# Neighbourhood attention on items of two heads by 16 grid columns, with the outputs read by the merge through a view

## The reference

```python
def row_fn(r):
    ...
    s_loc = jnp.einsum('bhqd,bhiqjd->bhqij', qr, kn) * scale + bias
    s_ctx = jnp.einsum('bhqd,bhmd->bhqm', qr, kc) * scale
    ...
    s = jnp.concatenate([s_loc.reshape(bsz, hh, wq, kh * NA_KW), s_ctx], axis=-1).astype(jnp.float32)
    p = jax.nn.softmax(s, axis=-1).astype(v.dtype)
    ...
    return jnp.einsum('bhqij,bhiqjd->bhqd', p_loc, vn) + jnp.einsum('bhqm,bhmd->bhqd', p_ctx, vc)
```

## Time and profile before

| | us |
|---|---|
| median of 3 runs | 2396.49 (2395.66 to 2397.57) |
| the profiled execution's own time | 2396.7 |
| its span, first to last instruction | 2394.9 |
| PE busy | 2350.3 (98%) |
| DVE busy | 1614.3 (67%) |
| ACT busy | 965.6 (40%) |
| POOL busy | 126.5 (5%) |
| mean granted clock of PE | 0.997 |

### The profile page before, as it was taken

How to read it: one execution, slowest core, us unless ns; L and a number is a source line. 1 busy time by engine, 2 the same in 40 slices (tenths; PEclk the granted TensorE clock), 3 DMA queues, 4 the chain that set the end, 5 groups by cost and what they waited for, 6 DMA issues and landing times.

```text
span 2394.9 us, 33087 instructions
## 1 busy us (share of the span) xinstructions
PE 2350.3 (98%) x13244; PEld 2034.2 (85%) x13244; DVE 1614.3 (67%) x2135; ACT 965.6 (40%) x1453; POOL 126.5 (5%) x158
## 2 busy tenths in 40 slices
PE   7999999999999999999999999999999999999998
PEld 4988988998877888898889888889889896998996
DVE  7677658856378545686766786766688556678656
ACT  2422356743136322353224464224567323544443
POOL 1000001101100000010000010000011010000000
PEclk9999999999999999999999999999999999999999
DMA  8655555652133344444456575456556243676763
GB/s 281 182 170 177 187 193 165 194 179 68 50 110 89 123 132 135 156 134 158 163 172 202 175 220 166 158 172 197 185 184 204 90 133 100 214 253 197 223 202 123
DMA packets 466300, 396.26 MB, mean 165 GB/s; under 512 B 34132, under 2 KB 418148, under 8 KB 465892
## 3 DMA queue, kind: packets, MB, share of 16 engines
q1 hardware_dynamic: 450704, 386.98, 51.3%
q10 hardware_dynamic: 15444, 7.17, 1.1%
HBM read 392.93 MB, written 1.17 MB: 165 GB/s over the span
## 4 chain that ended last, share of the span: by engine, by line
PE 89%; DVE 7%; issue 1%; DMA 1%; ACT 1%; ACTq 0%; POOL 0%; SPq 0%; DVEq 0%
PE ps L1648 27%; PE ps L1650 27%; PE ps L1649 27%; DVE wl L1031 2%; PE ps L1945 1%; PE ps L2021 1%; PE ps L2000 1%; PE ps L2104 1%; DVE st L1099 1%; DMA araw<-in_ada_w 1%; PE ps L1755 1%; PE ps L1926 1%; PE ps L2009 1%; ACT wh L590 1%; DVE acc L1046 0%
## 5 line engine op out<-in xcount | busy, mean ns | idle before, releaser
L1031 DVE TENSOR_TENSOR wl<-raw,wh 128x1024 fp32r<-128x1024 f32 x560 | 681.4, 1221 | 561.3 <-ACT wh L590 559.5
L590 ACT ACTIVATE wh<-raw 128x1024 fp32r<-128x1024 f32 x560 | 591.7, 1059 | 1147.4 <-PE ps L1650 1078.9
L1648 PE MATMUL ps<-hh,wh 128*128 128x256 f32 (+1 forms) x2720 | 883.9, 325 | 1.1 <-DVE hl L1204 0.7
L1649 PE MATMUL ps<-hl,wh 128*128 128x256 f32 (+1 forms) x2720 | 880.2, 324 | 0.0
L1650 PE MATMUL ps<-hh,wl 128*128 128x256 f32 (+1 forms) x2720 | 880.1, 324 | 0.0
L1648 PEld LDWEIGHTS ps<-hh,wh 128*128 128x128 f32 x2720 | 517.8, 190 | 43.4 <-issue 1.7
L1650 PEld LDWEIGHTS ps<-hh,wl 128*128 128x128 f32 x2720 | 517.6, 190 | 40.9
L1649 PEld LDWEIGHTS ps<-hl,wh 128*128 128x128 f32 x2720 | 517.8, 190 | 40.4
L1046 DVE SCALAR_TENSOR_TENSOR acc<-araw,c,acc 128x1024 f32<-128x1024 f32 x210 | 258.7, 1280 | 54.6 <-DMA araw<-in_ada_w 53.1
L1648 PE MATMUL ps<-wh,stage_h_f 128*128 128x512 f32 x616 | 240.7, 391 | 2.0 <-DVE stage_l_f L1288 2.0
L1649 PE MATMUL ps<-wl,stage_h_f 128*128 128x512 f32 x616 | 239.8, 389 | 0.0
(11 more groups left out here) (201 smaller groups left out, 2328.1 us busy)
## 6 DMA issues: line engine op xcount, KB each, us to landing
raw<-in_ffa_w SPq DMA_DIRECT2D x204, 512.0 KB, 3.9
raw<-in_ffb_w SPq DMA_DIRECT2D x168, 512.0 KB, 3.8
raw<-in_mix_w_in SPq DMA_DIRECT2D x148, 512.0 KB, 4.3
araw<-in_ada_w SPq DMA_DIRECT2D x136, 512.0 KB, 5.2
raw<-in_ret_w_out SPq DMA_DIRECT2D x16, 512.0 KB, 4.8
raw<-in_na_fou_w_out SPq DMA_DIRECT2D x16, 512.0 KB, 4.0
raw<-in_mix_w_o SPq DMA_DIRECT2D x16, 512.0 KB, 3.9
raw<-in_ada_w SPq DMA_DIRECT2D x8, 512.0 KB, 5.6
```

The source lines that it names most:

```text
L590: A.activation(w_home(u)[0], raw[:, s, :], ACT.Copy).then_inc(w_rounded, 1)
L1031: V.tensor_tensor(low, raw[:, s, :], f(high), ALU.subtract).then_inc(w_split, 1)
L1648: T.matmul(out, a[0], b[0], start=start, stop=False)
L1649: T.matmul(out, a[0], b[1], start=False, stop=False)
```

## The change

- **Items.** An item is now a pair of heads, a stream and a tile j of 16 grid columns (16 columns by 4 rows by 2 heads = 128 queries). The counts stay: 32 items in layer 0, 16 in layer 1. A latent item takes the 32 columns around its tile (`WIN`), 128 keys, and the 256 context keys: 384 instead of 512, in two products of 128 and 256 columns. Context items keep 256 keys.
- **Token order.** Latent tokens are loaded and stored by column (`by_column`), and the rotary, Fourier and distance tables are permuted to match, so that a window of columns is contiguous. Context tokens are permuted too.
- **Values.** `nv` holds a window of 128 keys for each j and the two context tiles, without zero padding. ACT copies windows 0 and 3 and the context tiles (one 128x512 copy each instead of two 128x256), and issues four DMAs (`NV_PARTS`) inside SBUF that put windows 1 and 2 together. PE waits for them (`nv_window`) before the values of items j = 1 and 2. POOL's zeroing of `nv` is gone.
- **Outputs in item order.** A bank holds the four tiles of one pair and stream. In it only the blocks of a head's own partitions and queries count; ACT and DVE copy them in two 64x256 pieces each (`out_blocks`) after every four items, contiguous in the item's order (row, then column within the tile). The merge's products on (`ah`,`al`) read them in token order through `by_token`, whose innermost step is 16 elements (64 bytes).
- **Queries.** ACT writes `nq` with a step of 16 elements.
- **Bias.** The table holds for each head, row difference and query column the four windows. It is written by 8 DMAs of 1920 rows of 128 bytes (before: 2 of 120 rows of 512 bytes), and the wait for it is moved from step 16 to step 24 of the first feed-forward block. Loading takes one DMA a head with rows of 512 bytes, each pair has its own buffer, SP no longer waits for items before it loads heads 4 to 7, and POOL masks four times a layer instead of eight.
- **Merge splits.** Rounding and splitting of the merge's first four units move from loop steps n-4, n-3, n-2, n-1 to n-5, n+1, n+2, n+3 (n is the number of items).

```diff
+QC, WC = 16, 32
+NQ = GRID_W // QC
+WIN = tuple(min(max(QC * j - 8, 0), GRID_W - WC) for j in range(NQ))
+LOCAL = WC * ROWS
...
-        n_items = [[(2 * pr + a, s, q) for pr in range(NH // 2) for s in range(2 if l < DEPTH - 1 else 1) for q in range(LT) for a in range(2)]
-                   for l in range(DEPTH)]
+        n_items = [[(pr, s, j) for pr in range(NH // 2) for s in range(2 if l < DEPTH - 1 else 1) for j in range(NQ)] for l in range(DEPTH)]
...
+        NV_PARTS = [(j, src, max(ROWS * (WIN[j] - w), 0), min(ROWS * (WIN[j] + WC - w), P), max(ROWS * (w - WIN[j]), 0))
+                    for j in range(1, NQ - 1) for src, w in ((0, WIN[0]), (NQ - 1, WIN[-1]))]
+        def out_blocks(y, outs, item, a):
+            pr, s, _ = item
+            p = slice(DH * a, DH * a + DH)
+            y = y[p].rearrange("p (j b q) -> p b j q", b=2, q=DH)[:, a]
+            return y, [o[p, pr, s * SEQ:(s + 1) * SEQ].rearrange("p (j q) -> p j q", q=DH) for o in outs]
+        def merge_at(l):
+            n = len(n_items[l])
+            return (n - 5, n + 1, n + 2, n + 3)
...
-            for r in range(ROWS):
-                row = (l * NH + h) * RPB_R + 7 - r
...
+            row = (l * NH + h) * RPB_R + RPB_R // 2 - (ROWS - 1)
+            src = bass.AP(tab.tensor, offset=row * QC * NQ * WC, ap=[[NQ * WC, ROWS * QC], [QC * NQ * WC, ROWS], [1, NQ * WC]])
+            queue.dma_start(bias[DH * (h % 2):DH * (h % 2) + DH, h // 2], src).then_inc(bias_in[h // 2], 16)
...
+                sp.wait_ge(r_fin, r0[l] + len(r_items[l]))
+                sp.wait_ge(tab_in, 16 * DEPTH * NQ)
                 for h in range(4, NH):
-                    sp.wait_ge(n_max, n0[l] + len(n_items[l]) // 4 * (h // 2 - 2) + 3 + h % 2)
                     load_bias(sp, l, h)
...
-                        act.dma_start(tab[l].rearrange("h r c -> (h r) c"), pad[:, l, :]).then_inc(tab_in, 16)
+                        for j in range(NQ):
+                            act.dma_start(tab[l, :, :, j * WC:(j + 1) * WC], pad_window(l, j)).then_inc(tab_in, 16)
+                elif q == KF + 2:
+                    act.wait_ge(tab_in, 16 * DEPTH * NQ)
                 elif q == HEAD + 7 + DEPTH:
-                    act.wait_ge(tab_in, 16 * DEPTH)
...
-                    if 0 <= t - (len(items) - RING) < RING:
-                        rounded(AT["merge", l] + t - (len(items) - RING))
+                    if t in merge_at(l):
+                        rounded(AT["merge", l] + merge_at(l).index(t))
...
-                    if t >= 5 and (t - 4) % (2 * per) == 0:
-                        pr = (t - 4) // (2 * per) - 1
-                        act.wait_ge(n_out, b + 2 * per * (pr + 1))
-                        A.copy(ah[:, pr, 0:N], ps[:, 4 + pr % 2, 0:N]).then_inc(n_hi, 1)
+                    if t >= 5 and (t - 4) % NQ == 0:
+                        grp = (t - 4) // NQ - 1
+                        act.wait_ge(n_out, b + NQ * (grp + 1))
+                        for a in range(2):
+                            y, o = out_blocks(ps[:, 4 + grp % 2], (ah,), items[NQ * grp], a)
+                            ins = A.copy(o[0], y)
+                        ins.then_inc(n_hi, 1)
...
-                    link(V.tensor_tensor(y[:, 0:SEQ], y[:, 0:SEQ], bias[:, h % 4, q], ALU.add))
+                        w = y[:, 0:LOCAL].rearrange("p (c r) -> p r c", r=ROWS)
+                        link(V.tensor_tensor(w, w, bias[:, pr, :, j * WC:(j + 1) * WC], ALU.add))
...
+            def by_token(w):
+                return w.rearrange("p (b r c) -> p b c r", r=ROWS, c=QC)
...
-                                (src[0][:, kt, n0:n], src[1][:, kt, n0:n]), kt == 0, kt == kts - 1)
+                                (view(src[0][:, kt, n0:n]), view(src[1][:, kt, n0:n])), kt == 0, kt == kts - 1)
...
-                    T.matmul(ps[:, SCORE_BANKS[t % 3], 0:key_n(items[t])], nq[:, q_slot(h), c:c + P],
-                             nk[:, h // 2, s * SEQ:TOK], start=True, stop=True).then_inc(n_score, 1)
+                        T.matmul(bank[:, 0:LOCAL], q, nk[:, pr, ROWS * WIN[j]:ROWS * WIN[j] + LOCAL], start=True, stop=True)
+                        T.matmul(bank[:, LOCAL:LOCAL + CTX], q, nk[:, pr, SEQ:TOK], start=True, stop=True).then_inc(n_score, 1)
...
-                    form_a(v + 3, 3, (ah, al), N, kts=4, last=False)
+                    form_a(v + 3, 3, (ah, al), N, kts=4, last=False, view=by_token)
```

More of the change, by code:

```diff
@@ L380, in trunk @@
         n0 = [0, len(n_items[0])]
+        g0 = [0, len(n_items[0]) // NQ]
+        groups = [len(items) // NQ for items in n_items]
         f0 = [0, len(f_items[0])]
@@ L782, in attention @@
                 items, b = n_items[l], n0[l]
-                per = len(items) // NH
                 for t in range(len(items) + 5):
@@ L1472, in maximum @@
                 def maximum(t):
-                    h, s, q = items[t]
+                    pr, s, j = items[t]
                     y = ps[:, SCORE_BANKS[t % 3]]
@@ L1497, in attention @@
                         low(6, 2)
-                    if t >= 5 and (t - 4) % (2 * per) == 0:
-                        pr = (t - 4) // (2 * per) - 1
-                        dve.wait_ge(n_hi, 4 * l + pr + 1)
-                        V.tensor_tensor(al[:, pr, 0:N], ps[:, 4 + pr % 2, 0:N], f(ah[:, pr, 0:N]), ALU.subtract).then_inc(n_lo, 1)
-                    if 0 <= t - (len(items) - RING) < RING:
-                        split(AT["merge", l] + t - (len(items) - RING))
+                    if t >= 5 and (t - 4) % NQ == 0:
+                        grp = (t - 4) // NQ - 1
+                        dve.wait_ge(n_hi, g0[l] + grp + 1)
+                        for a in range(2):
+                            y, (high, low_) = out_blocks(ps[:, 4 + grp % 2], (ah, al), items[NQ * grp], a)
+                            ins = V.tensor_tensor(low_, y, f(high), ALU.subtract)
+                        ins.then_inc(n_lo, 1)
+                    if t in merge_at(l):
+                        split(AT["merge", l] + merge_at(l).index(t))
             def copy_in(dst, u, idx):
@@ L2012, in values @@
                 def values(t):
-                    h, s, q = items[t]
-                    pr = h // 2
+                    pr, s, j = items[t]
+                    grp = t // NQ
                     pe.wait_ge(n_turnc, b + t + 1)
-                    if t % (2 * per) == 0 and pr >= 2:
-                        pe.wait_ge(n_lo, 4 * l + pr - 1)
-                    c = s * SEQ + q * P
-                    kts = list(range(NT) if s == 0 else range(LT, NT))
-                    for j, kt in enumerate(kts):
-                        ins = T.matmul(ps[:, 4 + pr % 2, c:c + P], nv[:, kt, h], probT[:, t % 2, j * P:(j + 1) * P],
-                                       start=j == 0 and h % 2 == 0, stop=j == len(kts) - 1 and h % 2 == 1)
+                    if j == 0 and grp >= 2:
+                        pe.wait_ge(n_lo, g0[l] + grp - 1)
+                    if s == 0 and 0 < j < NQ - 1:
+                        pe.wait_ge(nv_window, 16 * len(NV_PARTS) * (l + 1))
+                    kts = ([j] if s == 0 else []) + [NQ, NQ + 1]
+                    for m, kt in enumerate(kts):
+                        ins = T.matmul(ps[:, 4 + grp % 2, j * P:(j + 1) * P], nv[:, kt, pr * P:(pr + 1) * P], probT[:, t % 2, m * P:(m + 1) * P],
+                                       start=m == 0, stop=m == len(kts) - 1)
                     ins.then_inc(n_out, 1)
                 pe.wait_ge(nq_zero, 2 * l + 2)
-                pe.wait_ge(nv_zero, l + 1)
                 for t in range(len(items) + 4):
```

100 lines of the change are left out of this document (51 added, 49 removed).

## The result

The changed kernel takes 2400.7 us (median of 12 runs, 2399.8 to 2403.4) against 2395.4 us (12 runs, 2393.4 to 2397.6) for the kernel before on the same chip: ratio 1.0024, 95% interval 1.0017 to 1.0032. The forecast was 2387.0 and faster. The result lies inside the range, but on the other side of no change.

The account below looks back on a forecast made before the run. The prediction took PE to pace both attentions, with DVE close behind. Layer 0 -3.5, layer 1 -6.7 and table +0.5 made -9.7 us against 2396.7: 2387.0 us, range 2378 to 2424.

Parts of the forecast that it names:

- Table: First feed-forward block: 15360 small writes cost each DMA engine 26 us of some 110; between nothing and 3 us, taken as +0.5.
- Rival 4: First feed-forward block: table writes take over 100 us, hold ACT at step 24 or delay weights; +5 to +10, chance 0.05.
- View: Merge: 96 matmuls a layer read `ah` or `al` with a 64-byte step; taken as costing nothing, the least certain term.
- the second rival: Merge: the view slows PE, +29.6 us at the fp32 passes' pace (2416.6 in all) or +48.7 at DVE's; chance 0.38.
- Layer 0: Attention, layer 0: DVE takes over as the pace, a turn takes 12.8 us; net -3.5 us.
- The first turn: Attention, layer 0: the turn without `al` runs at PE's 11.0 us and saves 2.4.
- the wait for `ol`: Second merge unit: PE waits for the second piece of `ol`, some 0.5 us in layer 0 and 1.6 in layer 1.
- Layer 1: Attention, layer 1: items at PE 1.65 and DVE 1.50 us, second merge unit starts at 2036.7 instead of 2045.0; net -6.7 us.
- Splits: End of the attentions: three of four splits leave the items, at 2.35 us a split, but are late for the next units.
- Bias add: Attention: DVE's add on scores read and written with a step of 4 elements, taken as 0.29 us.
- `nq`, `nv`: Attention: ACT's stepped `nq` writes fit even at 1 us each; the window DMAs of `nv` cost nothing.

Follow-up runs that it names:

- e2: The changed kernel with the merge reading `ah` and `al` in place, without the view: 2394.7 us, ratio 0.9999.
- e9: The changed kernel with its table writes spread as in e1 and a different run length and step of reading in each merge column block: 2397.3 us (one run).
- e1: The changed kernel with its eight table writes issued one behind each step from 13 to 20 of the first feed-forward block: 2390.8 us, ratio 0.9982.
- e7: The changed kernel with spread table writes, queries in column-first order, no view, and DVE's `al` copies one item later: 2378.3 us, ratio 0.9927.
- e3: The changed kernel with the roundings and splits of the first four merge units back at items n-4 to n-1: 2405.3 us, ratio 1.0043.
- e5: The kernel before with only the merge's first four roundings and splits moved as in the change: 2391.8 us, ratio 0.9986.

## Why the prediction was wrong

*Table: the step that failed.* The prediction counted what the 15360 rows cost the DMA engines, found 26 us of 110, and took 0.5 us. As a bound that count was sound: the queue's share of the span rose from 1.1% to 1.5% only, with 24766 packets, and neither 27 ns nor the doubled price that the prediction considered shows in the 14 ns of a packet. What it left out is that ACT issues the writes itself and stands still meanwhile. The queues and waits were gone through for every other step; here only the transfer was priced, not its issuing. Measured: 19.9 us of issuing, PE's gap of 7.3 and 2.7 of lowered clock, which make 10.0 of the 10.3 us. Rival 4 named ACT and the weights and +5 to +10, but at step 24, by waiting for the writes to land; the hold was at step 13, and nothing showed at 24. With 0.05 it was badly underrated: it alone turned the sign.

*View: the least certain term, taken at its lower end.* Forecast nothing, measured 4.0 and 1.4 us from the records, 6.0 by e2. That is nearer to nothing than to the upper bounds of 29.6 and 48.7, but only because ROWS is 4: with runs of 8 the price would have been 0.21 us a matmul, just the second rival's. The argument for nothing (no row has PE held back by a read) was the absence of a row, not a measurement. "Below nothing is excluded" was no measurement either: e9's runs of 2 took 0.216 us against 0.227 in place. Without the table this term alone would have left the change at e1's 2390.8, faster by 0.18%.

*Layer 0: size off by half.* Forecast -3.5, measured -1.7, and of these 0.75 are the lowered clock in the trace before. The turn was 13.9 us, not 12.8. From the start of a scaling to the next add an `al` now takes 749.28 - 747.12 = 2.16 us, some 1.85 more than without, where 1.45 was taken: DVE waits 0.91 or 0.74 us for ACT, which has two copies of `ah` to make first. That is 0.8 of the 1.1 a turn; the rest is short waits for PE, as the 0.23 in the rows above. The first turn (forecast 11.0, measured 10.6) and the wait for `ol` (0.5 and 0.6) were about right. That DVE and no longer PE sets the pace was right, and e7 shows it.

*Layer 1: better than forecast,* -8.4 instead of -6.7. PE's 1.65 and DVE's 1.51 us an item came out; less the shift of 10.8 us the second unit starts at 2035.5 (forecast 2036.7), and the wait for `ol` was 1.1 instead of 1.6.

*Splits.* Forecast as part of the attentions, at 2.35 us for each split among the items; e3 puts their place at 4.6 us of the gain, and in its trace 3.1 of 4.0 us are lowered clock, which the prediction had nowhere. How much of it needs the short items e5 leaves open (3.4 us by its runs, 1.2 by its trace).

*Bias add and `nq`, `nv`:* 0.29 us as taken; `nq`'s stepped writes took 0.62 to 0.69 us each and hid behind an idle ACT; nothing waited for the windows of `nv`.

In sum: the attentions gave 10.1 us where 10.2 were forecast (the errors of the two layers cancel, which is luck), the merges took 5.5 where nothing was forecast, the table 10.3 where 0.5 was.

## What to carry to other kernels

A DMA has two prices: the engines that move it, and the engine that issues it. Price both, and ask what that engine's silence starves; here eight writes of 1920 rows in one burst held the issuer for 19.9 us, at the pace of the transfer, and the same writes, one a step, cost nothing. When items get shorter, look at the copies that come once in a group: a wait that was covered by PE's surplus can set the pace afterwards, and moving its consumer by one item was worth 7.5 us here, more than the 4.4 us of the change with its table spread (e1). Look at the granted clock in every stretch that is compared: short waits of PE may be followed by microseconds at half clock, and the cost then shows in the work behind them. And measure a strided read before it is built in.

## What the runs showed of the hardware that was not expected

PE's moving operand (fp32r, width 512) may be read in runs of 2 at a step of 16 elements, or backwards, for 0.216 and 0.234 us against 0.227 in place; runs of 4 cost 0.27 (0.34 at step 2), runs of 8 and more 0.43 to 0.48. ACT's queue took two writes of 1920 rows at 1.0 and 1.5 us and then held its engine for 1.7 to 3.9 us for each of the other six. In a gap of 7.3 us the granted clock fell to 0.50, and work went on at that level for 5.7 us; in e3 it fell to 0.50 for 6.8 us behind waits of PE of 0.8 to 1.7 us. DVE added 128 scores a row, read and written in PSUM at a step of 4 elements, in 0.29 us; contiguous ones would take as much by an estimate from the 0.43 us for 256 and 1.07 ns an element.
